# Two-block forward pass on one core: second expert layer with rows moved by indirect DMA and four 32-row blocks side by side; scale chunks of the modulation first

## The reference, cut to what matters

```
mx = silu(c) @ w_ada[l] + b_ada[l];  sh1, sc1, ga1, sh2, sc2, ga2 = split(mx, 6)
px = modulate(rmsnorm(x, g_norm1), sh1, sc1) @ w_in[l]      # h * (1 + scale) + shift
pc = modulate(rmsnorm(ctx, g_norm1), csh1, csc1) @ w_in[l]
```

```
g_star = argmax(softmax(hf @ wg + bg));  e_sel = (hf @ we + be)[g_star]
top_v, top_i = top_k(softmax(e_sel), 2);  weights = p_gsel * top_v / sum(top_v)
y[n] = sum over e of combine[n, e] * (silu(hf @ w_gate[e]) * (hf @ w_up[e])) @ w_down[e]
out = rmsnorm(x + y, norm_final_g)
```

## Time and profile before

| what | value |
|---|---|
| median of 3 runs | 2169.39 us (2168.69 to 2171.74) |
| the profiled execution, its own time | 2166.3 us |
| its span, first to last instruction | 2164.4 us |
| mean granted TensorE clock | 0.959 |
| PE busy | 1996.4 us, 92% of the span |
| VectorE, ScalarE, GpSimd busy | 733.9, 470.2, 12.6 us |
| DMA | 399.03 MB, mean 184 GB/s |

### The profile page before, as it was taken

The page is one execution under the profiler, slowest core; times in us unless marked ns, Lnnn a source line. Parts: engine busy times, 40 slices in busy tenths (PEclk is TensorE's granted clock), DMA queues, the critical chain, the costliest instruction groups (busy, mean ns, idle before and its releaser), DMA issues.

```text
span 2164.4 us, 19621 instructions
## 1 busy us (share of the span) xinstructions
PE 1996.4 (92%) x7415; PEld 921.1 (43%) x7415; DVE 733.9 (34%) x1355; ACT 470.2 (22%) x845; POOL 12.6 (1%) x17
## 2 busy tenths in 40 slices
PE   6899999999899999999997997899997859999997
PEld 3544545544364444344433442344444334444443
DVE  3606205521231111111113695210212255455554
ACT  3211114420211110010112006530003222323223
POOL 0000000000000000000000000000000020000000
PEclk7999999999999999999998997999998969999999
DMA  9111443113238999999980211111200048878862
GB/s 371 28 66 39 173 177 136 39 59 117 78 122 349 422 417 419 422 422 422 423 345 18 72 66 39 40 39 62 72 22 0 0 151 289 296 273 288 293 233 78
DMA packets 151110, 399.03 MB, mean 184 GB/s; under 512 B 9284, under 2 KB 75156, under 8 KB 142868
## 3 DMA queue, kind: packets, MB, share of 16 engines
q1 hardware_dynamic: 144636, 393.40, 48.0%
q10 hardware_dynamic: 6424, 4.94, 0.7%
HBM read 396.23 MB, written 2.10 MB: 184 GB/s over the span
## 4 chain that ended last, share of the span: by engine, by line
PE 88%; DVE 4%; ACT 3%; issue 1%; DMA 1%; SPq 0%; DVEq 0%; ACTq 0%
PE bank L1529 49%; PE bank L1852 10%; PE bank L2099 6%; PE bank L1876 5%; PE bank L1827 3%; PE bank L1898 3%; PE bank L2121 3%; DVE SM L582 1%; PE bank L574 1%; PE bank L1980 1%; PE bank L2065 1%; PE bank L1605 1%; PE bank L1727 1%; PE bank L1560 1%; DMA weight_slots<-in_expert_w_up 1%
## 5 line engine op out<-in xcount | busy, mean ns | idle before, releaser
L1529 PE MATMUL bank<-H,weight_slots 128*128 128x512 f32 (+1 forms) x1088 | 450.0, 574 | 13.7 <-ACT H L620 12.5
L1529 PEld LDWEIGHTS bank<-H,weight_slots 128*128 128x128 f32 x1088 | 208.9, 193 | 252.6 <-issue 247.3
L1529 PE MATMUL bank<-R,weight_slots 128*128 128x512 f32 x576 | 249.1, 593 | 4.4 <-DVE R L1158 2.1
L1529 PEld LDWEIGHTS bank<-R,weight_slots 128*128 128x128 f32 x576 | 109.0, 190 | 141.6 <-issue 134.6
L1852 PE MATMUL bank<-weight_slots,SM 128*64 128x512 f32 x640 | 141.8, 593 | 6.8 <-DVE xT L1221 6.8
L2099 PE MATMUL bank<-weight_slots,SM 128*64 128x512 f32 x512 | 136.3, 622 | 5.6 <-DMA weight_slots<-in_expert_w_up 5.6
L1471 DVE TENSOR_TENSOR xT<-xT,bank 128x512 f32<-128x512 f32 x136 | 91.6, 686 | 78.8 <-PE bank L1529 78.8
L1876 PE MATMUL bank<-weight_slots,SM 128*64 128x512 f32 x384 | 111.6, 594 | 0.0
L1529 PE MATMUL bank<-R 128*128 128x128 f32 (+2 forms) x784 | 103.3, 287 | 3.2 <-ACT R L874 2.1
L1529 PEld LDWEIGHTS bank<-R 128*128 128x128 f32 x784 | 94.2, 195 | 7.1 <-issue 4.6
L1852 PEld LDWEIGHTS bank<-weight_slots,SM 128*64 128x64 f32 x640 | 45.4, 137 | 100.1 <-issue 86.7
(11 more groups left out here) (386 smaller groups left out, 2057.0 us busy)
## 6 DMA issues: line engine op xcount, KB each, us to landing
weight_slots<-in_w_up_e SPq DMA_DIRECT2D x24, 2048.0 KB, 12.7
weight_slots<-in_w_down_e SPq DMA_DIRECT2D x24, 2048.0 KB, 20.8
weight_slots<-in_w_in SPq DMA_DIRECT2D x18, 2048.0 KB, 10.2
weight_slots<-in_w_gate_e SPq DMA_DIRECT2D x16, 2048.0 KB, 11.8
weight_slots<-in_expert_w_gate SPq DMA_DIRECT2D x32, 1024.0 KB, 10.0
weight_slots<-in_expert_w_up SPq DMA_DIRECT2D x32, 1024.0 KB, 11.7
R<-in_expert_w_down SPq DMA_DIRECT2D x32, 1024.0 KB, 8.3
weight_slots<-in_w_ada SPq DMA_DIRECT2D x12, 2048.0 KB, 10.3
```

Of the source, the lines that this page charges most:

```text
L1529: ins = nc.tensor.matmul(dst, lhsT, rhs, start=(i == 0), stop=(i == len(pairs) - 1))
```

## The change

**Start.** The order of the four first chunks becomes 2, 3, 0, 1 (scale first). `gains` waits for the first four `mods` only, ACT waits for the shift chunk of each half where it adds it. On PE, `wide_sum` of n1 stands ahead of the third chunk. The nine small DMAs go from ACT's queue to SP's, behind the eighth weight load.

**Second experts.** Blocks have 32 rows, at most 47 of them, in `NQUAD` = 12 steps ("quads") of four blocks. Column i of a quad is block 12 i + q: each of the four columns walks through its own run of blocks, and the experts of group i are moved into column i as far as room allows (`shift`). Four experts (0, 4, 8, 12) are loaded ahead of the routing; later loads carry a condition `changed` and are skipped where the column's expert stays the same. A slot is refilled in place, gate and up in halves of four k tiles; there is no second set. The rows of the activations are written to DRAM (`h2_rows`, 4 DMAs from ACT), gathered by 12 indirect DMAs of 128 rows on POOL, and turned by 8 transposes for each quad. Gate and up are 32 products and down 16, in four column tiles of 32. The weighted results go to DRAM (`y_rows`, one DMA for each quad from ACT), and at the end POOL adds them to the token-major x with 8 indirect DMAs of 128 rows that accumulate in SBUF. The final norm works on token-major rows: ACT squares, DVE scales, SP writes four outputs. The rounding into fp32r, the 0/1 gathers and the scatters are gone. All 12 quads are written out, without a loop.

```diff
-BLK = 64
+BLK = 32
+NQUAD = -(-((2 * T + E2 * (BLK - 1)) // BLK) // 4)
+ADA_CHUNK = (2, 3, 0, 1, 4, 5, 6, 7, 8, 9, 10, 11)
@@ sync
             for n, (name, src, free, value) in enumerate(W):
+                if n == 2 * NSLOT:
+                    small_weights()
...
+            def load_half(i, half, expert, changed=None):
                 for j, name in enumerate(("expert_w_gate_2", "expert_w_up_2")):
+                    src = A[name][0].rearrange("e (p k) n -> p e k n", p=P)[:, expert, 4 * half:4 * half + 4, :]
+                    dst = ring_jk[i][:, j:j + 1, 4 * half:4 * half + 4, :]
+                    sp.dma_start(dst, src, cond=changed).then_inc(sem(f"half{half}_in"), 16)
...
+            for q in range(1, NQUAD + 1):
+                ago = here
+                if q < NQUAD:
+                    here = [block_of_step(q, i) for i in range(NSLOT)]
+                    for half in range(2):
+                        sp.wait_ge(sem("gate_up_halves"), 2 * (q - 1) + half + 1)
+                        for i in range(NSLOT):
+                            load_half(i, half, *here[i])
+                if q > 1:
+                    sp.wait_ge(sem("down_halves"), 2 * (q - 1))
+                for i in range(1 if q == 1 else 0, NSLOT):
+                    load_down(i, *ago[i])
@@ vector
-                    dve.wait_ge(sem("b_gates"), pair + 1)
...
+            nc.vector.tensor_tensor(in_row, iota2..., row_of..., ALU.is_equal).then_inc(sem("one_hot"), 1)
+            dve.wait_ge(*reached("idx_mm", 1))
+            nc.vector.tensor_copy(slot_token[:, :], PS[4][:, 0:NQUAD]).then_inc(sem("slot_tokens"), 1)
@@ gpsimd
-                nc.gpsimd.tensor_tensor(h2_low[...], h2_all[...], full(h2_high[...]), ALU.subtract)
+                nc.gpsimd.indirect_dma_start(rows_in[q], None, h2_rows, bass.IndirectOffsetOnAxis(ap=slot_token[:, q:q + 1], axis=0))
...
+                    nc.gpsimd.indirect_dma_start(x_tok2[:, t, :], None, y_rows, bass.IndirectOffsetOnAxis(ap=token_slot[...], axis=0), compute_op=ALU.add)
@@ tensor
             ada_sum(0, ada_part0)
+            ada_sum(1, ada_part0)
+            wide_sum(pe, "n1", ...)
             ada(2)
-            ada_sum(1, ada_part0)
             ada(3)
...
+            for q in range(NQUAD):
+                pe.wait_ge(sem("q_xb"), 2 * (q + 1))
+                gate_up(q, 0)
+                if q:
+                    turn_hidden(q - 1)
+                gate_up(q, 1)
+                if q + 1 < NQUAD:
+                    turn_rows(q + 1)
+                if q:
+                    down(q - 1)
```

More of the change, by code:

```diff
@@ L96 @@
 SHARED = {"product_done": bases(PRODUCT_STAGES), "copy_done": bases(COPY_STAGES), "vector_done": bases(VECTOR_STAGES)}
-CONST = {"ident": 0, "ones": 128, "s_le_j": 256, "s_ge_j": 384, "future": 512, "dft": 640, "iota": 896, "pick": 960, "fold": 962}
-NCONST = 982
+CONST = {"ident": 0, "ones": 128, "s_le_j": 256, "s_ge_j": 384, "future": 512, "dft": 640, "iota": 896, "pick": 960, "fold": 962, "token": 982, "ahead": 986, "column": 991, "first": 995}
+NCONST = 999
 def constant_tables():
@@ L323, in build @@
         xrec = tokg[:, 224:240].rearrange("p (h i) -> p h i", h=4)
-        h2_high, h2_low = (rounded_in(f"h2_{part}", where, column, 4096).rearrange("p (t d) -> p t d", t=TT)
-                           for part, where, column in (("high", "R6", 0), ("low", "R14", 4096)))
-        h2_all = R14[:, 0:4096].rearrange("p (t d) -> p t d", t=TT)
+        h2_stage = R6[:, :].rearrange("p (t d) -> p t d", t=TT)
+        zeros16 = R5[0:E2, 0:T]
         chosen = rowsB[0:E2, :]
@@ new lines, in _ @@
+            for q in range(NQUAD):
+                if q:
+                    hidden_turned(q - 1)
+                silu(q)
+                if q:
+                    y_out(q - 1)
+            hidden_turned(NQUAD - 1)
+            y_out(NQUAD - 1)
+            for t in range(TT):
+                act.wait_ge(sem(f"sum_in{t}"), 32)
+                act.activation(last_sq, x_tok2[:, t, :], ACT.Square, accum_out=out_ss[:, t:t + 1]).then_inc(sem("out_sq"), 1)
+                act.wait_ge(sem("out_sq"), t + 1)
+                act.activation(out_std[:, t:t + 1], out_ss[:, t:t + 1], ACT.Sqrt, bias=small[:, 40:41], scale=1.0 / D).then_inc(sem("out_root"), 1)
@@ new lines, in _ @@
+            for q in range(NQUAD):
+                if q + 1 < NQUAD:
+                    x_turned(q + 1)
+                hidden(q)
+            dve.wait_ge(sem("g_out_in"), 16)
+            for t in range(TT):
+                dve.wait_ge(sem("out_root"), t + 1)
+                nc.vector.reciprocal(out_rstd[:, t:t + 1], out_std[:, t:t + 1]).then_inc(sem("out_inverse"), 1)
+                dve.wait_ge(sem("out_inverse"), t + 1)
+                nc.vector.scalar_tensor_tensor(out=out_tok[:, t, :], in0=x_tok2[:, t, :], scalar=out_rstd[:, t:t + 1], in1=g_out,
+                                               op0=ALU.mult, op1=ALU.mult).then_inc(sem("out_ready"), 1)
@@ new lines, in down @@
+            def down(q):
+                pe.wait_ge(sem("down_in"), 16 * (4 * (q + 2) - 1))
+                pe.wait_ge(sem("q_hidT"), q + 1)
+                if q:
+                    pe.wait_ge(sem("q_y"), 2 * q)
+                for half in range(2):
+                    for f in range(2):
+                        c = 1024 * f + 512 * half
+                        for i in range(4):
+                            r = slice(BLK * i, BLK * (i + 1))
+                            ins = nc.tensor.matmul(PS[6 + half][r, :], hbT[:, f, r], down_s[:, i, c:c + 512], start=(f == 0), stop=(f == 1), tile_position=(0, BLK * i))
+                    ins.then_inc(sem("down_halves"), 1)
@@ L2142 @@
+            turn_hidden(NQUAD - 1)
+            down(NQUAD - 1)
 def kernel(**inputs):
```

528 lines of the change are left out of this document (257 added, 271 removed).

## The result

The changed kernel takes **1982.22 us** (median of 4 runs, 1980.61 to 1983.51), the kernel before beside it 2169.3; the ratio is 0.9135, 95% interval 0.9119 to 0.9151. Measured a second time (experiment 5) it took 1983.6 us. The forecast was 1975.0: right in direction and place, 7 us too low.

The account below looks back on a forecast made before the run. PE, busy 92% of the span, was taken as the bound. Gains of 13 at the start, 178 through router stage and loop, and 0 at the end sum to 191: 2166.3 - 191 = 1975 us, own range 1938 to about 2045.

Parts of the forecast that it names:

- Start: Up to PE's first projection: small DMAs off ACT and n1's sums earlier gain 13 us, bounds 8.3 and 20.5.
- Router stage: From 1735 us to the first gate and up: 6 us gained after new steps, bounds 12 and -6.
- the clash of GpSimd and VectorE: Router stage: POOL's subtractions slow nine small VectorE operations, losing 5.5 us that the change wins back.
- A quad: Second experts' loop: PE needs 13.1 us, SP 13.6; 13.5 us taken for each of twelve, bounds 12 and 16.
- I take the issue into a free queue: SP in a quad: a skipped load priced like an issue into a free queue, twenty at 0.42 us.
- Weights: Second experts' loop: 14 expert changes of 7.5 us each, mostly hidden behind quads, cost 19 us, bounds 0 and 105.
- weights exposed: Rival for the loop: every expert change is waited for, 105 us in place of 19, total 2061 us; chance 0.12.
- End: After the last down: 30 us, with eight gathers at 2.5 each, so 0 us gained, bounds -10 and +27.
- The estimate of 26: End: the skill's GpSimd DMA cost, eight accumulating gathers in series, 26 us and the kernel 6 us later.
- Skipped loads that hold SP: Rival for the loop: a skipped load costs 1.0 us of queue, a quad 25 us, total 2115 us; chance 0.10.
- Narrow tiles two at a time: Rival on PE: 0.228 us an instruction, 23.5 us a quad, total 2095 us; chance 0.04.
- The skip that saves nothing: Slower rival: all 48 column loads move, 35.6 us a quad, total 2221 us; chance 0.04.

Follow-up runs that it names:

- experiment 5: The changed kernel run once more with no edit: 1983.6 us, ratio 0.9149.
- E2: The kernel before with only the whole edit of the start (chunk order, n1's sums earlier, small DMAs on SP): 2149.16 us, ratio 0.9913.
- E9: The changed kernel with GpSimd's eight subtractions put back into the router stage, their result unused: 1990.4 us, ratio 0.9185.
- E4: The changed kernel with all change flags written as 1, so every conditional load moves its data: 2194.96 us, ratio 1.0122.
- E3: The changed kernel with all change flags written as 0, so no expert is reloaded in the loop: 1939.15 us, ratio 0.8943.
- E12: The changed kernel with the edits of E6 and E7, plus SP reading the next quad's table entries ahead: 1973.27 us, ratio 0.9100.
- E11: The changed kernel with only the first two of its twelve row gathers: 1977.6 us, ratio 0.9125.
- E6: The changed kernel with each gather from the fourth on waiting for gate and up of the quad three before: 1981.38 us, ratio 0.9142.
- E7: The changed kernel with the end's eight accumulating gathers replaced by plain ones, summed by VectorE: 1980.21 us, ratio 0.9132.
- E1: The kernel before with only its nine small DMAs moved from ScalarE's queue to SP's: 2157.8 us, ratio 0.9958.

## Why the prediction was right, and where it was not

**Start, 13 us taken: 18.3 in the trace, 19.2 by E2.** The mechanism and the releaser are as forecast, and the bounds (8.3 and 20.5) hold it. The size failed at the clock: chunks 0 and 1 were priced at the low-clock 3.64 of the earlier trace rows and ran in 1.92, their sums at 3.6 and ran in 1.95. Together these are 5.1 of the 5.3 us missed.

**Router stage, 6 us taken: 3.4.** The 5.5 for the clash of GpSimd and VectorE is confirmed by E9 (4.9 on VectorE, 6.8 in the whole). The forecast's sum here can't be followed to its 1771: it names the new steps, but not what they replace. The traces do it: from PE's counts to the first gate and up the kernel before took 23.7 us (1753.67 to 1777.34, the last 5.57 a wait for weights), the changed one 25.6 (from 1730.01, with the first gather 17.3 after it). So 5.4 us are gained ahead of the counts and 2.0 lost behind them.

**A quad, 13.5 us taken: 12.0.** On PE 0.114 us an instruction, not 0.12, and starts overlap a little: 12.0 for the 13.1 of the sum. No drain at a change of tiling mode is visible, as far as modelled ends can show it: in the slower kernel of E4 the two transposes follow the tiled product's 5.49 us at 1923.65, 0.07 before its modelled end. The rule of the Trainium skill, "TensorEngine Tiling (Array Packing)", Key Properties, cost nothing that these traces show. On SP the step "I take the issue into a free queue" failed: a skipped load is 0.17 us with its gap, not 0.42, so a quad on SP is about 10 us and never paces (E3). Over twelve quads and the last steps: 166.5 forecast, 145.0 measured, 21.5 gained.

**Weights, 19 us taken: 46.** This is the step that failed. The count (14) and the places were exact; the price of a change was not. The forecast took 7.5 us of transfer against 13.5 us of cover, so that a single change cost 1 us, two 1.5 and three 9. The three cost 12; the other eleven, priced at 10 us together, cost some 34. Four things were missing or too small: the cover is only 12.0 (for a first half 8.3, from one first half's end to the next one's start in E3; the forecast's 8.6 does not follow from its own 13.5); in six quads the first half's refill starts 1.7 to 4.1 us after PE frees it, since SP loads down and reads its table first (reading ahead gained about 4 us in E12); the loads share the engines with the gathers (about 6 us in all, E11); and the long waits bring the lower clock with them, 11 us in five groups of products. How the 27 us missed divide among the four isn't shown. Even so, 46 is less than half of the 105 of the rival "weights exposed". E6 and E11 show too that a gain in one quad comes back in part as a wait in the next, so that the terms of this stage can't be added up one by one.

**End, 30 us taken: 35.2.** The gathers were priced at 2.5 us each, 20; they took 25.1. The estimate of 26 that the Trainium skill, "DMA: Bandwidth & Descriptors", Anatomy of one DMA, led to came out nearer, and the kernel is 5.6 us slower there for the 6 it gave. But not as it was reckoned, one after the other: the median gather lands 9.6 us after its issue, several are under way at once, and the DMA engines are full for 19 us at 205 GB/s. The figure that failed is the rate: the forecast's shortest time, 10 us, had 422 GB/s in it, and even E7 with plain gathers reaches 358. Why accumulation halves it was not tested. That the estimate of 26 came within 1 us is chance.

**The sum.** Errors of +5.3 at the start, -2.6 in the router stage, +21.5 in the quads, -26.9 in the weights and -5.6 at the end leave -8.3: 191 forecast, 182.7 by the spans. The time was close because two terms of over 20 us cancelled, which is luck in good part: the loop as a whole was 185.5 forecast and 190.9 measured. The two may belong together, since a quad that is faster has less to hide a change behind; no run slows the quad to show it.

**The rivals.** Skipped loads that hold SP: out, by a factor of six in their price. Narrow tiles two at a time: out. The skip that saves nothing: not the case, 350.13 MB for E4's 453.95; made so, it costs 26 us over the kernel before, not 52. Weights exposed: a part of it.

## What to carry to other kernels

When data-dependent work skips its transfers, price the transfers that remain from the place where the slot becomes free: what the issuing queue has to read first, what shares the DMA engines then, and what the wait does to TensorE's clock. Reckon a stage once with these transfers taken out and once with all of them made (here 145 and 397 us): the real one lies between, and the two show at once whether compute or transfer is the limit. A faster inner step leaves less cover for what runs beside it, so the estimate for the one has to be put into the estimate of the other. A gather that accumulates should be priced by its own rate, and compared with a plain one whose sums another engine makes.

## What the runs showed of the hardware

- A skipped conditional load costs 0.07 us of the queue and 0.17 to the next, where the forecast had 0.42 an issue.
- The page's "HBM read" seems to count skipped loads: 467.02 MB in the changed kernel, in E3 and in E4 alike, while q1 moved 350.13, 306.09 and 453.95 MB. The queue's own row is the one to read.
- An indirect gather of 128 rows of 4 KB is 0.94 us of GpSimd's time, with accumulation 1.54; each then 0.30 us apart.
- With the DMA engines full (share 0.96 and more), plain gathers moved 358 GB/s (E7) and accumulating ones 205 (the changed kernel).
- PE's granted clock in the first 40 us differs between executions and kernels: the chunk of 16 products at 35.44 us took 3.64 in the kernel before (granted clock 0.50) and 1.92 at 35.51 in E1 (1.00), where nothing ahead of it on PE was changed. Why was not tested.
